# Turning a recurrence's outputs between the last gate tiles instead of behind them

## The chip, the cores and the metric

The kernel runs on one core of one Trainium2 chip. The metric is the device time of one execution in microseconds (us); a kernel's time is the median of its runs.

## The reference, cut to what matters

A first block mixes 512 tokens of width 1024 in four branches, gates and adds them, and is followed by two further layers. The change lies in branch A, a recurrence over four heads of 64 columns, and in what happens to its outputs:

```python
o = wkv7(rh, heads(decay), kh, vh, -kk, kk * ah)
o = layer_norm(o, lnx_w.reshape(H_A, HEAD_A), lnx_b.reshape(H_A, HEAD_A), LNX_EPS)
o = o + jnp.sum(rh * kh * r_k, axis=-1, keepdims=True) * vh
return (o.reshape(bsz, seq, D_MIX) * g) @ w_out, v_first
...
merged = (gates[:, :, 0] * y_a + gates[:, :, 1] * y_b + gates[:, :, 2] * y_c + gates[:, :, 3] * y_d)
x = x + gt1 * (merged @ w_o[l])
```

The norm is over the 64 columns of a head, for each token and head; its weight and bias are one number for each of the 256 columns.

## The kernel before

Activations lie with columns on the 128 partitions and 512 tokens in the free dimension. A matrix product is done in pieces: a piece is 1024 columns of weights for 128 partitions (512 KB), which makes one output tile of 128x512 from 8 blocks of 128 rows, or four output tiles from 2 blocks each (the branches' own output weights). Each block takes three products (high times high, high times low, low times high; L1602, in product_steps), so a piece is 24 products of 512 columns. Output tiles go round four PSUM banks, 0 to 3; a tile waits until its bank was read.

The weights come over GpSimd's queue in the order of the pieces, into four slots: load_high fetches a piece (L440), load_low negates it into the low half (L446) and adds it again by an accumulating transfer (L449). The first product of a piece frees the slot of the piece before it, and load_high of the third piece ahead waits for that; GpSimd works in order, so the low half of the piece after next is issued only behind it.

Ahead of the recurrence, blocks (L1916) does small products of 128 rows and 64 columns of weights, with outputs on the lower and the upper 64 partitions in turn. The recurrence goes over 16 chunks of 32 tokens (VectorE's loop L711, TensorE's with L1961 to L1982). Between its small products TensorE does gate tiles and branch tiles in steps (the generator named beside, L1937), and VectorE the gating of finished tiles in steps of its own (beside, L691, called by step_beside, L703). In VectorE's case 32 steps are to be done in 40 calls, so the last eight calls do nothing. ScalarE copies each chunk's outputs out of PSUM into the tile o (L1433), which has (head, token in the chunk) on the 128 partitions and (chunk, column) in the free dimension: 128x1024.

Behind the recurrence, TensorE does four gate tiles (project(4, "gate"), L1987), called gate tiles 1 to 4 here. Meanwhile VectorE norms o: mean, centred o, square, variance (L735 to L740), ScalarE's square root (L1468, in order behind the gate tiles left from the recurrence), reciprocal and scaling (L742, L743), then the norm's weight and bias, which lie repeated over 64 columns each in the tile vec (L746, L747). Then o is written twice, masked by the parity of the head (L750), and 32 TensorE products with 64 rows and 128 columns of weights, moved by 32 columns, turn it to columns on partitions (L1993; 64 instructions, since a product in plain float32 is two). VectorE adds the bonus, multiplies by g and splits into a high and a low half, for two tiles of 128x512 (L753, L754, L481, L482). This is the tail.

Then branch_out(3, 8) (L1998) makes the branch's eight output tiles from two pieces, here output pieces 1 and 2. VectorE gates each (L1112), adds it to the sum of the branches (L1121) and splits the sum in two (L481, L482), 4 instructions for each of 8 tiles. The first tile of the next projection (w_o, L1999) takes these halves as they come, and the other seven follow. SyncE fetches x again in four parts as the sum's tiles are done (L410).

Of the kernel before, what the change touches and what calls it, by code (L numbers as in the profile page):

```python
# [20 lines left out]
AX = mybir.AxisListType  # L21

P = 128
T = 512
# [3 lines left out]
H_A, HD = 4, 64  # L28
C = 32
NCK = T // C  # L30
# [57 lines left out]
def vec_columns():  # L88

    sizes = [("c", 8), ("ada_b", 48), ("g_mix", 8), ("mu", 7), ("w0", 2), ("a0", 2), ("kk", 2), ("ka", 2), ("rk", 2),  # L90
             ("sg_w", 2), ("sg_b", 2), ("conv_w", 6), ("s5_d", 2), ("a_re", 8), ("a_im", 8), ("log_dt", 8),
             ("g_ffn", 8), ("g_final1", 8), ("g_mix2", 16), ("g_mem2", 16), ("g_ffn2", 16), ("b_f", 1),
             ("cw2", 2 * 3 * 44), ("cb2", 2 * 44), ("g_final", 8), ("lnx_w", 64), ("lnx_b", 64)]
    at, cols = 0, {}
    for name, n in sizes:
        cols[name] = (at, n)
        at += n
    return cols, at


VEC, NVEC = vec_columns()


# [67 lines left out]
def build(nc, A, out):  # L171
# [15 lines left out]
    with ExitStack() as ctx:  # L187
# [5 lines left out]
        def S(name):  # L193
            if name not in sems:
                sems[name] = ctx.enter_context(nc.semaphore(name))
            return sems[name]
# [4 lines left out]
        x = sb("x", [P, KT, T])  # L201
        h_hi = sb("h_hi", [P, KT, T], F32R)
        h_lo = sb("h_lo", [P, KT, T], F32R)
        g_hi = sb("g_hi", [P, KT, T], F32R)
        g_lo = sb("g_lo", [P, KT, T], F32R)
        work = sb("work", [P, 6, T])
        vec = sb("vec", [P, NVEC])
        con = sb("con", [P, NCON])
        mod = sb("mod", [P, 48])
        small = sb("small", [P, 40, 8])  # L210
# [7 lines left out]
        ps = [banks8[:, i, :] for i in range(8)]  # L218
# [13 lines left out]
        def K(name):  # L232
            at, size = CON[name]
            return con[:, at:at + size]

        def place(sizes, at=0):

            parts = {}
            for name, shape in sizes:
# [7 lines left out]
                elif len(shape) == 4:  # L247
# [7 lines left out]
        rw_pad = place([("a", (2, NCK, 2, C)), ("b", (2, NCK, 2, C)), ("k", (2, NCK, 2, C)), ("r", (2, NCK, 2, C)),  # L255
                        ("g", (2, T)), ("bonus", (2, T))])
# [6 lines left out]
        rw_sol = place([("as", (C, C)), ("z", (C // 2, C)), ("o", (NCK, 64))],  # L263
                       at=max(rw_in["end"], rw_bd["end"]))
# [10 lines left out]
                     at=base_at + 7 * T)  # L275
# [9 lines left out]
                          at=sol_at))  # L285
# [181 lines left out]
        def _(dve):  # L467
            n = Counts()

            def do(ins, name="dve_step"):  # L470

                ins.then_inc(S(name), 1)
                dve.wait_ge(S(name), n.next(name))

            def need(name, by=1):

                dve.wait_ge(S(name), n.next(name, by))

            def both_parts(hi, lo, src, name):

                do(dve.tensor_copy(hi, src))  # L481
                do(dve.tensor_tensor(lo, src, hi.bitcast(F32), ALU.subtract), name)  # L482
# [112 lines left out]
            def vector_recurrence():  # L595

                v, bd, sol = rw_in, rw_bd, rw_sol
# [93 lines left out]
                def beside():  # L691

                    skip(8)
                    for f in range(4):
                        yield from gate_steps(4 + f)
                    for f in range(KT):
                        if f % 2 == 0:
                            skip(1)
                        yield from gate_steps(f, glu_tiles=True)

                steps, turn = beside(), [0]

                def step_beside():  # L703

# [24 lines left out]
                    pass  # L729
                need("rec_o")  # L730
                need("rec_o_copied", 2 * NCK)
                o, sq = sol["o"], bd["ab"]
                mean, var = small[:, 29:31, :].rearrange("p a b -> p (a b)"), small[:, 31:33, :].rearrange("p a b -> p (a b)")
                spread = lambda s: s.unsqueeze(2).broadcast_to((P, NCK, HD))
                do(dve.tensor_reduce(mean, o, AX.X, ALU.add))  # L735
                do(dve.tensor_scalar(mean, mean, 1.0 / HD, None, ALU.mult))
                do(dve.tensor_tensor(o, o, spread(mean), ALU.subtract))
                do(dve.tensor_tensor(sq, o, o, ALU.mult))
                do(dve.tensor_reduce(var, sq, AX.X, ALU.add))
                do(dve.tensor_scalar(var, var, 1.0 / HD, LNX_EPS, ALU.mult, ALU.add), "rw_var")  # L740
                need("rw_std")
                do(dve.reciprocal(var, var))  # L742
                do(dve.tensor_tensor(o, o, spread(var), ALU.mult))  # L743
                at_w, at_b = VEC["lnx_w"][0], VEC["lnx_b"][0]
                over = lambda at: vec[:, at:at + HD].unsqueeze(1).broadcast_to((P, NCK, HD))
                do(dve.tensor_tensor(o, o, over(at_w), ALU.mult))  # L746
                do(dve.tensor_tensor(o, o, over(at_b), ALU.add))  # L747
                opad = rw_pad["a"].rearrange("p a n h c -> p (a n h c)").rearrange("p (n h i) -> p n h i", n=NCK, h=2)
                for g in range(2):
                    do(dve.tensor_scalar(opad[:, :, g, :], o, K("hm")[:, g:g + 1], None, ALU.mult), "o_padded")  # L750
                for k in range(2):
                    need("rw_o")
                    do(dve.tensor_tensor(rw_pad["bonus"][:, k], rw_pad["bonus"][:, k], ps[4 + k][:], ALU.add))  # L753
                    do(dve.tensor_tensor(rw_pad["bonus"][:, k], rw_pad["bonus"][:, k], rw_pad["g"][:, k], ALU.mult))  # L754
                    both_parts(g_hi[:, 6 + k, :], g_lo[:, 6 + k, :], rw_pad["bonus"][:, k], "rw_out")
                skip(8)

            def vector_layer(layer):
# [257 lines left out]
            f = [blocks4(m["f"][:, part]) for part in range(2)]  # L1016
# [51 lines left out]
            while L < NQ:  # L1068
                over = lambda v: v.unsqueeze(2).broadcast_to((P, S5T, L))
# [505 lines left out]
        def _(pe):  # L1575
            n = Counts()
            piece, t = [0], [0]
# [71 lines left out]
            h = (of(h_hi), of(h_lo))  # L1649

            def project(tiles, owner, operand=h, width=T, blocks=8, ready=None):

                for i in range(tiles):
                    slot = open_piece()
                    product(slot, blocks, *operand, owner if isinstance(owner, str) else owner[i], width,
                            ready=ready if i == 0 else None)
# [157 lines left out]
            for k in range(2):  # L1814
                mm = pe.matmul(PA[:], K("ones"), m["z"][:, 2 + k, :], start=(k == 0), stop=(k == 1))
            mm.then_inc(S("sg_sums"), 1)
            project(1, "s5_u")
            for k in range(2):
                need("sg_square")
                mm = pe.matmul(PB[:], K("ones"), m["sq"][:, k, :], start=(k == 0), stop=(k == 1))  # L1820
            mm.then_inc(S("sg_sums"), 1)
            project(1, "dve_freed")
            for k in range(2):
                need("sg_normed")
                for b in range(QB):
                    mm = pe.transpose(ps[6 + k][:, P * b:P * b + P], m["z"][:, 2 + k, P * b:P * b + P], K("ident"))
# [16 lines left out]
            for s in range(S5T):  # L1843
                for part in range(2):
                    for g in range(2):
                        mm = pe.matmul(ps[4 + part][halves[g], NQ * s:NQ * s + NQ], m["e"][:, part, s, halves[g]], m["u_turned"][:, 2 * s + g, :],
                                       start=True, stop=True)
# [3 lines left out]
            for s in range(S5T):  # L1851
                for g in range(2):
                    pe.matmul(ps[6 + g][:, NQ * s:NQ * s + NQ], m["toep"][:, 2 * s + g].rearrange("p j c -> p (j c)"), m["u_turned"][:, 2 * s + g, :],
                              start=(s == 0), stop=False, skip_group_check=True)
            need("s5_states")
            for s in range(S5T):
                for part in range(2):
                    for g in range(2):
                        mm = pe.matmul(ps[6 + g][:, NQ * s + 1:NQ * s + NQ], m["g"][halves[g], part, s, :],
                                       m["w"][halves[g], part, NQ * s:NQ * s + NQ - 1], start=False,  # L1860
                                       stop=(part == 1 and s == S5T - 1), skip_group_check=True)
# [122 lines left out]
                next(steps, None)  # L1984
            for _ in steps:
                pass
            project(4, "gate")  # L1987
            pe.wait_ge(S("o_padded"), 2)
            opad = rw_pad["a"].rearrange("p a n h c -> p (a n h c)").rearrange("p (n x) -> p n x", n=NCK)
            for p in range(2):  # L1990
                rows = slice(64 * p, 64 * p + 64)
                for c in range(NCK):
                    mm = pe.matmul(ps[4 + p][:, C * c:C * c + C], opad[rows, c, :], K("sum32")[rows, :], start=True, stop=True)  # L1993
                mm.then_inc(S("rw_o"), 1)


            pe.wait_ge(S("rw_out"), 2)
            branch_out(3, 8)  # L1998
# [71 lines left out]
def columns(v):  # L2070

    return v.reshape(-1, P).T
# [34 lines left out]
def layout(i):  # L2107
# [21 lines left out]
    for layer, w in ((0, i["w_in_fox_2"][0]), (1, i["w_in_dil_2"][0])):  # L2129
# [14 lines left out]
        for n in FF2_GROUPS:  # L2144
# [11 lines left out]
           "b_f": np.concatenate([i["b_forget_2"][0], np.zeros(P - NH, np.float32)])[:, None],  # L2156
           "cw2": columns(i["conv_w_2"].reshape(-1)), "cb2": columns(i["conv_b_2"].reshape(-1)),
           "g_final": columns(i["norm_final_2"]),
           "lnx_w": np.repeat(f["rwkv_lnx_w"].reshape(H_A, HD), C, axis=0), "lnx_b": np.repeat(f["rwkv_lnx_b"].reshape(H_A, HD), C, axis=0)}
    b = np.stack([f["s5_b_re"], f["s5_b_im"]])  # L2160
    c = np.stack([f["s5_c_re"], f["s5_c_im"]])
    arrays = dict(
# [20 lines left out]
```

## Time and profile before

| | us |
|---|---|
| median of three runs | 2294.26 (2290.89 to 2295.56) |
| the profiled execution | 2292.73 |
| its span, first to last instruction | 2290.7 |
| TensorE busy | 2137.2, 93% of the span |
| VectorE busy | 1297.5, 57% |
| GpSimd busy | 843.6, 37% |
| ScalarE busy | 455.8, 20% |
| mean granted TensorE clock | 0.964 of full speed |

Rows give start and duration in us from the start of the span. A line L1602 is a line of the kernel, and stands for every call of a helper that it belongs to. The idle time in square brackets is that of the engine just before the instruction, with what ended it. TensorE (PE) overlaps its products, so the step from one start to the next tells its pace, not the duration; weight loads have rows of their own (PEld). Granted clock 1.00 is 2.4 GHz and 0.50 is 1.2 GHz.

### The profile page before, as it was taken

What the parts mean: (1) busy time and instruction counts of PE and PEld (TensorE: products, weight loads), DVE (VectorE), ACT (ScalarE), POOL (GpSimd) and SP (SyncE); (2) the same over time, 40 slices, a digit from 0 to 9 for tenths busy, and PEclk for the clock granted to TensorE, in tenths of its full rate; (3) what the DMA queues carried; (4) which work ended last, traced back from release to release, by engine and by line L of the source; (5) the groups of instructions that cost most, each with busy time, mean ns of one, the idle gap of its engine ahead of it and who ended that gap; (6) DMA issues with size and microseconds to landing.
All of it is one profiled execution on the core that took longest, in us unless ns stands there. A gap on an engine that the chain in (4) does not pass through costs nothing.

```text
span 2290.7 us, 27377 instructions
## 1 busy us (share of the span) xinstructions
PE 2137.2 (93%) x10790; PEld 1697.7 (74%) x10790; DVE 1297.5 (57%) x1824; ACT 455.8 (20%) x839; POOL 843.6 (37%) x1009
## 2 busy tenths in 40 slices
PE   6989799998799999989999999999989979999996
PEld 4768586676588888876767888888766658888885
DVE  7775655436763243684444754737746656727365
ACT  2112301220100000213332211102223432202011
POOL 1323233332244444442213444444432224444442
PEclk7999899998899999999999999999999989999998
DMA  8868577576799899975437889888964538888885
GB/s 289 231 134 173 114 142 148 120 175 167 237 233 195 191 198 190 194 170 127 102 74 171 188 192 195 189 197 170 201 134 100 103 81 187 189 196 192 194 186 126
DMA packets 121783, 389.40 MB, mean 170 GB/s; under 512 B 25220, under 2 KB 27396, under 8 KB 121272
## 3 DMA queue, kind: packets, MB, share of 16 engines
q0 software_dynamic: 96624, 346.27, 69.8%
q1 hardware_dynamic: 25032, 41.39, 5.4%
q8 instruction: 86, 1.41, 0.2%
q14 instruction: 41, 0.34, 0.1%
HBM read 383.73 MB, written 3.92 MB: 169 GB/s over the span
## 4 chain that ended last, share of the span: by engine, by line
PE 79%; DVE 12%; DMA 5%; issue 1%; ACT 1%; POOL 1%; SPq 0%; DVEq 0%; ACTq 0%
PE ps L1602 65%; DMA w_lo<-in_w 2%; PE ps L1730 2%; PE ps L1631 2%; PE ps L1759 2%; DMA arena<-in_ada 1%; PE ps L1745 1%; PE ps L1916 1%; DMA w_hi<-in_w 1%; DVE work L688 1%; DVE g_lo L482 1%; DVE arena L689 1%; DVE small L875 1%; DVE work L536 1%; DVE h_lo L532 0%
## 5 line engine op out<-in xcount | busy, mean ns | idle before, releaser
L1602 PE MATMUL ps<-h_hi,w_hi 128*128 128x512 f32 x1760 | 712.3, 405 | 28.7 <-DVE h_lo L532 13.3
L1602 PE MATMUL ps<-h_lo,w_hi 128*128 128x512 f32 x1760 | 691.0, 393 | 0.0
L1602 PE MATMUL ps<-h_hi,w_lo 128*128 128x512 f32 x1760 | 690.8, 392 | 0.0
L440 POOL DMA_DIRECT2D w_hi<-in_w x334 | 185.9, 557 | 1258.7 <-PE ps L1602 1190.4
L1602 PEld LDWEIGHTS ps<-h_hi,w_hi 128*128 128x128 f32 x1760 | 333.4, 189 | 127.5 <-issue 30.1
L1602 PEld LDWEIGHTS ps<-h_hi,w_lo 128*128 128x128 f32 x1760 | 333.3, 189 | 71.8
L1602 PEld LDWEIGHTS ps<-h_lo,w_hi 128*128 128x128 f32 x1760 | 334.0, 190 | 65.0 <-issue 2.2
L446 POOL TENSOR_SCALAR w_lo<-w_hi 128x1024 fp32r<-128x1024 f32 (+1 forms) x334 | 357.5, 1070 | 55.6 <-DMA w_hi<-in_w 50.2
L449 POOL DMA_DIRECT2D w_lo<-in_w x334 | 300.6, 900 | 105.7 <-POOL w_lo L446 105.7
L1602 PE MATMUL ps<-g_hi,w_hi 128*128 128x512 f32 (+1 forms) x792 | 310.9, 393 | 15.8 <-DVE g_lo L482 6.0
L1602 PE MATMUL ps<-g_lo,w_hi 128*128 128x512 f32 (+1 forms) x792 | 304.7, 385 | 0.0
L1602 PE MATMUL ps<-g_hi,w_lo 128*128 128x512 f32 (+1 forms) x792 | 304.5, 384 | 0.0
L1602 PEld LDWEIGHTS ps<-g_hi,w_hi 128*128 128x128 f32 x792 | 151.4, 191 | 51.2 <-DMA w_lo<-in_w 8.5
L1602 PEld LDWEIGHTS ps<-g_hi,w_lo 128*128 128x128 f32 x792 | 151.1, 191 | 29.5
L1602 PEld LDWEIGHTS ps<-g_lo,w_hi 128*128 128x128 f32 x792 | 151.4, 191 | 28.2 <-issue 0.5
L1560 ACT ACTIVATE arena<-arena,vec 128x512 f32<-128x512 f32 x88 | 71.8, 816 | 395.2 <-DVE arena L921 391.9
L935 DVE TENSOR_TENSOR x<-ps,x 128x512 f32<-128x512 f32 x48 | 33.2, 691 | 148.0 <-PE ps L1602 137.7
L921 DVE TENSOR_TENSOR arena<-ps,work 128x512 f32<-128x512 f32 x88 | 60.8, 691 | 94.8 <-PE ps L1602 93.4
L926 DVE SCALAR_TENSOR_TENSOR arena<-arena,vec 128x511 f32<-128x511 f32 x88 | 112.6, 1279 | 3.3 <-ACT arena L1560 0.3
L1190 DVE TENSOR_TENSOR arena<-arena 128x512 f32<-128x512 f32 x32 | 53.9, 1683 | 71.1 <-ACT arena L1481 71.1
L1198 DVE SCALAR_TENSOR_TENSOR x<-ps,mod,x 128x512 f32<-128x512 f32 x32 | 24.0, 750 | 102.2 <-PE ps L1602 102.1
L481 DVE CAST g_hi<-arena 128x512 fp32r<-128x512 f32 (+1 forms) x100 | 79.1, 791 | 3.4
(373 smaller groups left out, 2068.3 us busy)
## 6 DMA issues: line engine op xcount, KB each, us to landing
w_hi<-in_w POOLq DMA_DIRECT2D x318, 512.0 KB, 4.0
w_lo<-in_w POOLq DMA_DIRECT2D x318, 512.0 KB, 5.7
arena<-in_ada SPq DMA_DIRECT2D x40, 512.0 KB, 8.5
w_hi<-in_w POOLq DMA_DIRECT2D x16, 384.0 KB, 3.5
w_lo<-in_w POOLq DMA_DIRECT2D x16, 384.0 KB, 5.0
x<-in_ada SPq DMA_DIRECT2D x8, 512.0 KB, 7.2
x<-in_xT SPq DMA_DIRECT2D x1, 2048.0 KB, 9.9
x<-in_xT SPq DMA_DIRECT2D x4, 512.0 KB, 4.1
```

What stands on the lines that cost most here:

```text
L440: pool.dma_start(w_hi[:, q % SLOTS, 0:n], A["w"][q][:, 0:n]).then_inc(S(f"high_in{q % SLOTS}"), 16)
L446: pool.tensor_scalar(w_lo[:, q % SLOTS, 0:n], w_hi[:, q % SLOTS, 0:n].bitcast(F32), -1.0, 0.0, ALU.mult, ALU.add).then_inc(S("negated"), 1)
L449: pool.dma_start(w_lo[:, q % SLOTS, 0:n], A["w"][q][:, 0:n], accum_op=ALU.add).then_inc(S(f"low_in{q % SLOTS}"), 16)
L481: do(dve.tensor_copy(hi, src))
L921: do(dve.tensor_tensor(cv_m["z"][:, side, :], tile()[:], rstd, ALU.mult), "conv_scaled")
L926: do(dve.scalar_tensor_tensor(dst[:, 1:], z[:, :T - 1], w(1), dst[:, 1:], ALU.mult, ALU.add))
L1190: do(dve.tensor_tensor(s, r, r, ALU.mult), "relu_used")
L1560: do(act.activation(c[:, j % 2, :], cv_m["z"][:, side, :], ACT.Identity, scale=V("cw2", at), bias=V("cb2", 44 * layer + 22 * side + j0 + j ...
L1602: mm = pe.matmul(bank, w[:, slot, cols], a(k), start=(k == 0 and i == 0), stop=(k == blocks - 1 and i == 2))
L1631: mm = pe.matmul(banks[i], w[:, slots[i], cols], a(k), start=(k == 0 and j == 0), stop=(k == blocks - 1 and j == 2))
L1730: mm = pe.matmul(ps[2 + g][:, 0:width], at_m["q"][half(g), pair, P * qb:P * qb + P], keys, start=True, stop=not fox)
L1759: mm = pe.matmul(ps[6][64 * g:64 * g + 64, P * qb:P * qb + P], values, at_m["pt"][:, u % 2, g, P * b:P * b + P], start=(b == 0), stop=(b = ...
```

## The change

Three things are done. VectorE's steps beside the recurrence get four more: mean, centred o, square and sum of squares of chunks 0 to 7 (centred(0)); the same of chunks 8 to 15 follows the recurrence. The turning products move from behind gate tile 4 to behind gate tile 2, and take another form: o's 64 columns of one chunk, all 128 rows, are the weights, and the 64 columns of the identity that belong to one parity of heads are moved through; 32 products again, two for each chunk, with their outputs on the upper and the lower 64 partitions in turn. The masked copies of o (L750) fall away. The norm's weight and bias are one column each for the two tiles of the tail, where they ride on its instructions, and the tile vec is 124 columns narrower. The tail waits for all 32 products and then has, for each of two tiles, two instructions of 256 columns and one of 512 before the two of the split.

```diff
@@ vec_columns, L93
-             ("cw2", 2 * 3 * 44), ("cb2", 2 * 44), ("g_final", 8), ("lnx_w", 64), ("lnx_b", 64)]
+             ("cw2", 2 * 3 * 44), ("cb2", 2 * 44), ("g_final", 8), ("lnx_w", 2), ("lnx_b", 2)]
@@ vector_recurrence, L701
-                steps, turn = beside(), [0]
+                o, sq = sol["o"], bd["ab"]
...
+                def centred(first):
+                    at = slice(first, first + NCK // 2)
+                    dve.wait_ge(S("rec_o_copied"), 2 * (first + NCK // 2))
+                    do(dve.tensor_reduce(mean[:, at], o[:, at], AX.X, ALU.add))
+                    yield
+                    do(dve.tensor_scalar(mean[:, at], mean[:, at], 1.0 / HD, None, ALU.mult))
+                    do(dve.tensor_tensor(o[:, at], o[:, at], mean[:, at].unsqueeze(2).broadcast_to((P, NCK // 2, HD)), ALU.subtract))
+                    yield
+                    do(dve.tensor_tensor(sq[:, at], o[:, at], o[:, at], ALU.mult))
+                    yield
+                    do(dve.tensor_reduce(var[:, at], sq[:, at], AX.X, ALU.add))
+                    yield
+                def all_beside():
+                    yield from beside()
+                    yield from centred(0)
+                steps, turn = all_beside(), [0]
@@ vector_recurrence, L732 to L755
-                do(dve.tensor_reduce(mean, o, AX.X, ALU.add))
-                do(dve.tensor_scalar(mean, mean, 1.0 / HD, None, ALU.mult))
-                do(dve.tensor_tensor(o, o, spread(mean), ALU.subtract))
-                do(dve.tensor_tensor(sq, o, o, ALU.mult))
-                do(dve.tensor_reduce(var, sq, AX.X, ALU.add))
+                for _ in centred(NCK // 2):
+                    pass
                 do(dve.tensor_scalar(var, var, 1.0 / HD, LNX_EPS, ALU.mult, ALU.add), "rw_var")
                 need("rw_std")
                 do(dve.reciprocal(var, var))
-                do(dve.tensor_tensor(o, o, spread(var), ALU.mult))
...
-                do(dve.tensor_tensor(o, o, over(at_w), ALU.mult))
-                do(dve.tensor_tensor(o, o, over(at_b), ALU.add))
-                opad = rw_pad["a"].rearrange("p a n h c -> p (a n h c)").rearrange("p (n h i) -> p n h i", n=NCK, h=2)
-                for g in range(2):
-                    do(dve.tensor_scalar(opad[:, :, g, :], o, K("hm")[:, g:g + 1], None, ALU.mult), "o_padded")
+                do(dve.tensor_tensor(o, o, var.unsqueeze(2).broadcast_to((P, NCK, HD)), ALU.mult), "o_normed")
+                need("rw_o", 2)
                 for k in range(2):
-                    need("rw_o")
-                    do(dve.tensor_tensor(rw_pad["bonus"][:, k], rw_pad["bonus"][:, k], ps[4 + k][:], ALU.add))
-                    do(dve.tensor_tensor(rw_pad["bonus"][:, k], rw_pad["bonus"][:, k], rw_pad["g"][:, k], ALU.mult))
-                    both_parts(g_hi[:, 6 + k, :], g_lo[:, 6 + k, :], rw_pad["bonus"][:, k], "rw_out")
+                    bonus = rw_pad["bonus"][:, k]
+                    for q in range(2):
+                        part = slice(T // 2 * q, T // 2 * q + T // 2)
+                        do(dve.scalar_tensor_tensor(bonus[:, part], ps[4 + q][:, T // 2 * k:T // 2 * k + T // 2], V("lnx_w", k), bonus[:, part],
+                                                    ALU.mult, ALU.add))
+                    do(dve.scalar_tensor_tensor(bonus, bonus, V("lnx_b", k), rw_pad["g"][:, k], ALU.add, ALU.mult))
+                    both_parts(g_hi[:, 6 + k, :], g_lo[:, 6 + k, :], bonus, "rw_out")
@@ TensorE's program, L1987 to L1997
-            project(4, "gate")
-            pe.wait_ge(S("o_padded"), 2)
-            opad = rw_pad["a"].rearrange("p a n h c -> p (a n h c)").rearrange("p (n x) -> p n x", n=NCK)
-            for p in range(2):
-                rows = slice(64 * p, 64 * p + 64)
-                for c in range(NCK):
-                    mm = pe.matmul(ps[4 + p][:, C * c:C * c + C], opad[rows, c, :], K("sum32")[rows, :], start=True, stop=True)
+            project(2, "gate")
+            pe.wait_ge(S("o_normed"), 1)
+            for q in range(2):
+                for c in range(NCK // 2):
+                    for g in range(2):
+                        columns_of = K("ident").rearrange("r (p h t) -> r p h t", p=2, h=2)[:, :, g, :]
+                        place_of = ps[4 + q][64 * g:64 * g + 64, :].rearrange("i (p n t) -> i p n t", p=2, t=C)[:, :, c, :]
+                        mm = pe.matmul(place_of, rw_sol["o"][:, NCK // 2 * q + c, :], columns_of, start=True, stop=True)
                 mm.then_inc(S("rw_o"), 1)
-
+            project(2, "gate")
```

## Rows read from the trace of the kernel before

**Rows 1.** The page: the chain that ended last, its shares of the span by engine.

```profile
PE 79%; DVE 12%; DMA 5%; issue 1%; ACT 1%; POOL 1%; SPq 0%; DVEq 0%; ACTq 0%
```

**Rows 2.** The chain of waits, 470 to 560 us: start us, us, what.

```profile
492.91 9.32 DMA w_lo<-in_w
...
502.27 16.66 PE ps L1602 x72
518.93 7.91 PE ps L1993 x64
...
556.17 4.21 PE ps L1602 x9
```

**Rows 3.** TensorE's timeline, 492 to 543 us: start us, us, engine, line, operation, [idle before, releaser].

```profile
507.66 0.39 PE L1602 MATMUL ps<-h_hi,w_lo 128*128 128x512 f32 x1
...
518.54 0.39 PE L1602 MATMUL ps<-h_hi,w_lo 128*128 128x512 f32 x1
...
529.58 0.80 PE L1602 MATMUL ps<-g_hi,w_hi 128*128 128x512 f32 x1 [2.76 <-DVE g_lo L482]
...
534.80 0.40 PE L1602 MATMUL ps<-g_hi,w_hi 128*128 128x512 f32 x1
```

**Rows 4.** Stretches: length, busy PE, PEld, DVE, ACT, POOL, granted clock, DMA share, GB/s.

```profile
304.00:306.00 2.00, 2.00 (x25) 1.67 (x20) 1.48 (x3) 0.00 (x0) 0.57 (x2) 1.00 0.81 213
...
524.00:525.00 1.00, 1.00 (x9) 1.00 (x8) 0.93 (x3) 0.00 (x0) 0.00 (x0) 0.74 0.00 0
```

**Rows 5.** TensorE's timeline at two groups of small products, 276 to 282 and 301 to 330 us.

```profile
277.13 3.68 PE L1916 MATMUL ps<-arena 128*64 128x64 f32 x64 [16.62 <-DVE arena L652]
...
302.40 2.09 PE L1916 MATMUL ps<-arena 128*64 128x64 f32 x64
304.42 0.50 PE L1602 MATMUL ps<-h_hi,w_hi 128*128 128x512 f32 x1
```

**Rows 6.** Line L1982 in the recurrence: duration ns min/median/max, first and last start, forms.

```profile
L1982 PEld LDWEIGHTS ps<-work,arena x52: 132/134/136, 406.2 to 487.7; 128*64 128x64 f32 x52
L1982 PE MATMUL ps<-work,arena x52: 222/246/270, 406.2 to 487.8; 128*64 128x64 f32 x52
```

**Rows 7.** VectorE's timeline, 486 to 560 us.

```profile
497.37 0.25 DVE L742 RECIPROCAL small<-small 128x16 f32<-128x16 f32 x1 [2.53 <-ACT small L1468]
497.65 1.23 DVE L743 TENSOR_TENSOR arena<-arena,small 128x1024 f32<-128x1024 f32 x1
...
526.92 0.69 DVE L753 TENSOR_TENSOR arena<-arena,ps 128x512 f32<-128x512 f32 x1 [1.60 <-PE ps L1993]
...
528.37 0.43 DVE L481 CAST g_hi<-arena 128x512 fp32r<-128x512 f32 x1
...
532.60 0.69 DVE L1112 TENSOR_TENSOR work<-ps,arena 128x512 f32<-128x512 f32 x1 [3.08 <-PE ps L1602]
...
546.37 1.83 DVE L482 TENSOR_TENSOR h_lo<-x,h_hi 128x512 fp32r<-128x512 f32 x1
...
555.42 0.69 DVE L482 TENSOR_TENSOR h_lo<-x,h_hi 128x512 fp32r<-128x512 f32 x1
559.97 0.75 DVE L1173 SCALAR_TENSOR_TENSOR x<-ps,mod,x 128x512 f32<-128x512 f32 x1 [3.86 <-DMA x<-in_xT]
```

**Rows 8.** GpSimd's timeline, 486 to 560 us.

```profile
510.52 0.89 POOL L449 DMA_DIRECT2D w_lo<-in_w  x1 [0.30 <-POOL w_lo L446]
...
530.68 0.55 POOL L440 DMA_DIRECT2D w_hi<-in_w  x1 [13.83 <-PE ps L1602]
...
546.59 1.06 POOL L446 TENSOR_SCALAR w_lo<-w_hi 128x1024 fp32r<-128x1024 f32 x1
```

**Rows 9.** VectorE's timeline in the recurrence's last steps.

```profile
478.54 0.22 DVE L719 COPY work<-ps 64x64 f32<-64x64 f32 x1 [1.63 <-PE ps L1969]
```

**Rows 10.** The page: DMA issues, KB each, median us from issue to landing.

```profile
w_lo<-in_w POOLq DMA_DIRECT2D x318, 512.0 KB, 5.7
...
vec<-in_vec SPq DMA_DIRECT2D x1, 335.0 KB, 2.9
```

More of the change, by code:

```diff
@@ L699, in beside @@
                         yield from gate_steps(f, glu_tiles=True)
-                steps, turn = beside(), [0]
+                o, sq = sol["o"], bd["ab"]
+                mean, var = small[:, 29:31, :].rearrange("p a b -> p (a b)"), small[:, 31:33, :].rearrange("p a b -> p (a b)")
+                def centred(first):
[14 more added lines that the diff above has]
+                steps, turn = all_beside(), [0]
                 def step_beside():
@@ L731, in vector_recurrence @@
                 need("rec_o_copied", 2 * NCK)
-                o, sq = sol["o"], bd["ab"]
-                mean, var = small[:, 29:31, :].rearrange("p a b -> p (a b)"), small[:, 31:33, :].rearrange("p a b -> p (a b)")
-                spread = lambda s: s.unsqueeze(2).broadcast_to((P, NCK, HD))
-                do(dve.tensor_reduce(mean, o, AX.X, ALU.add))
-                do(dve.tensor_scalar(mean, mean, 1.0 / HD, None, ALU.mult))
-                do(dve.tensor_tensor(o, o, spread(mean), ALU.subtract))
-                do(dve.tensor_tensor(sq, o, o, ALU.mult))
-                do(dve.tensor_reduce(var, sq, AX.X, ALU.add))
+                for _ in centred(NCK // 2):
+                    pass
                 do(dve.tensor_scalar(var, var, 1.0 / HD, LNX_EPS, ALU.mult, ALU.add), "rw_var")
@@ L742, in vector_recurrence @@
                 do(dve.reciprocal(var, var))
-                do(dve.tensor_tensor(o, o, spread(var), ALU.mult))
-                at_w, at_b = VEC["lnx_w"][0], VEC["lnx_b"][0]
-                over = lambda at: vec[:, at:at + HD].unsqueeze(1).broadcast_to((P, NCK, HD))
-                do(dve.tensor_tensor(o, o, over(at_w), ALU.mult))
-                do(dve.tensor_tensor(o, o, over(at_b), ALU.add))
-                opad = rw_pad["a"].rearrange("p a n h c -> p (a n h c)").rearrange("p (n h i) -> p n h i", n=NCK, h=2)
-                for g in range(2):
-                    do(dve.tensor_scalar(opad[:, :, g, :], o, K("hm")[:, g:g + 1], None, ALU.mult), "o_padded")
-                for k in range(2):
-                    need("rw_o")
-                    do(dve.tensor_tensor(rw_pad["bonus"][:, k], rw_pad["bonus"][:, k], ps[4 + k][:], ALU.add))
-                    do(dve.tensor_tensor(rw_pad["bonus"][:, k], rw_pad["bonus"][:, k], rw_pad["g"][:, k], ALU.mult))
-                    both_parts(g_hi[:, 6 + k, :], g_lo[:, 6 + k, :], rw_pad["bonus"][:, k], "rw_out")
+                do(dve.tensor_tensor(o, o, var.unsqueeze(2).broadcast_to((P, NCK, HD)), ALU.mult), "o_normed")
+                need("rw_o", 2)
+                for k in range(2):
+                    bonus = rw_pad["bonus"][:, k]
[5 more added lines that the diff above has]
+                    both_parts(g_hi[:, 6 + k, :], g_lo[:, 6 + k, :], bonus, "rw_out")
                 skip(8)
@@ L2158, in layout @@
            "g_final": columns(i["norm_final_2"]),
-           "lnx_w": np.repeat(f["rwkv_lnx_w"].reshape(H_A, HD), C, axis=0), "lnx_b": np.repeat(f["rwkv_lnx_b"].reshape(H_A, HD), C, axis=0)}
+           "lnx_w": columns(f["rwkv_lnx_w"].reshape(-1)), "lnx_b": columns(f["rwkv_lnx_b"].reshape(-1))}
     b = np.stack([f["s5_b_re"], f["s5_b_im"]])
```

## The prediction

> **What bounds the kernel now.** I read the chain of waits first. TensorE holds 79% of it and VectorE 12% [rows 1], so a change counts where TensorE stands still, runs slowly, or hands the chain to VectorE. All three happen behind the recurrence [rows 2]. A late weight transfer, 9.32 us long, holds gate tile 2 until 502.27. The gate tiles follow at 10.88/48 = 0.227 us a product, from the last product of tile 2 at 507.66 to the last of tile 4 at 518.54 [rows 3]. Then the 64 turning instructions take 7.91 us, to 526.84 [rows 2], 0.124 us each; TensorE stands 2.76 us for the tail on VectorE, and output piece 1 starts at 529.58 [rows 3]. The clock has been lost meanwhile: its mean is 0.74 in the sixth microsecond of the turning products [rows 4], and output piece 1's first product takes 0.80 us where the thirteenth, at 534.80, takes 0.40 [rows 3]. The twelve before that took 5.22 us instead of 12 x 0.227 = 2.72. VectorE gates the first output tile at 532.60 and from there holds the chain itself: its last instruction of the stretch ends at 555.42 + 0.69 = 556.11 [rows 7], and TensorE goes on at 556.17 [rows 2]. So the figure to follow is the 532.60. What comes after it hangs on events, not on a fixed time.
>
> **The turning products, moved and made anew.** Their new form has 128 rows, 64 columns of weights and 64 moved columns, with outputs on the two halves of the partitions in turn. The trace has just this shape at L1916: 64 instructions at 302.40, the next gate tile's product at 304.42, so 2.02 us [rows 5], with the clock at 1.00 behind them [rows 4]. New are a moving operand and an output in two runs of 32 columns; no row shows what that costs. Above, 7.91 us, today's form, bounds it; below, the 2.02 themselves, since split runs can hardly beat whole ones of the same shape and count. I take 2.02, the nearest row.
>
> The Trainium skill speaks against so low a price: "TensorE: Matmul & The Clock Gate", Back-to-back issue gap, gives a product of up to 64 columns about 62 ns where instructions are decoded in microcode. That would make 64 x 62 ns = 4.0 us, and the sum 2 us worse. L1916's 2.02/64 = 32 ns says that this does not bind here [rows 5].
>
> So the products start behind gate tile 2, at 507.66 + 0.39 = 508.05, and end at 510.07. They wait for the normed o, ready at 497.65 + 1.23 = 498.88 [rows 7], 9.2 us early. Gate tiles 3 and 4 then take 10.88 us and a first step about 0.1 longer: output piece 1 can start at 521.05, 8.5 us sooner. Of this 5.9 are the cheaper products and 2.7 the tail's wait, less that step.
>
> **The tail under gate tiles 3 and 4.** It begins at about 510.2 and has, for each of two tiles, two instructions of 256 columns, one of 512, a cast of 0.43 and a subtraction of 0.69 [rows 7]. The one with 512 is 0.75, by the same operation on PSUM at 559.97. Those of 256 lie between nothing and 0.75; I take 0.48. With gaps a tile is 3.0 us and the tail 6.0, done at 516.2, under cover until 521.05. GpSimd's negation can stretch a VectorE instruction from 0.69 to 1.83, as at 546.37 beside the one at 546.59 [rows 7, 8]; two such make 518.5, still covered. Without the cover the tail would cost its 6 us.
>
> **The clock.** With gate tiles right ahead, output piece 1 runs at full clock. VectorE got its first tile 3.02 us behind the piece's start; six products at 0.227, the last 0.39 long, and 0.1 for the signal make 1.6. VectorE starts at 522.7: 9.9 us sooner.
>
> **VectorE's stretch.** It took 23.5 us and still has its 32 instructions. Two of them were stretched by 1.14; a third negation came at 530.68 + 0.55 = 531.2 [rows 8], just before it. Now it comes at about 522.3 (1.1 + 0.55 behind output piece 1's start, less 0.4 for that product at full clock) and falls on the stretch's first two instructions. Nothing to +1.14; I take +0.6.
>
> For that third one the Trainium skill has a rule in "SBUF — State Buffer", Who interferes with whom: a VectorE instruction with at most one input in SBUF, outside the two-port modes, doesn't contend with GpSimd. The first, L1112, reads PSUM and SBUF and would go free, and the sum would be 0.6 better if the negation ended with it; no row settles the second.
>
> **The norm's halves.** Four new steps in VectorE's program fall into calls that did nothing. Each is half of an instruction of about 1.2 us, and VectorE stands 1.63 us at such a place [rows 9]. Should one be stretched, what queues behind it is a copy that TensorE reads only after six more products, 1.4 us. Cost nothing; bound from above 1 us. The gain is nothing too: the reciprocal waits for ScalarE's root [rows 7], which is in order behind a gate tile, and the normed o has 9.2 us to spare. L746, L747 and L750 fall away under the same cover.
>
> **Weights.** Output piece 1's low half is issued about 2.6 us behind the start of gate tile 3 (510.52 against 507.89) [rows 8] and lands in 5.7 [rows 10]: 8.3 us, where the new order leaves 11.0. With the 9.32 of rows 2 it would be 1 us late. The wait before gate tile 2 stays; shorter VectorE work beside GpSimd's negation might cut its 1.8 us, and a busier one lengthen it; I take nothing. The vec transfer is 124 of 670 columns shorter. Of its 2.9 us [rows 10] that is at most 0.5; I take 0.2, since other loads share the queue.
>
> **Sum.** -9.9 + 0.6 - 0.2 = -9.5 us, made against the profiled execution of 2292.73: 2283.2. The median of the runs is 1.5 above it, so 2284.8 on that base; I forecast 2284, between the two.
>
> **Rivals.**
> *The clock falls under the small products.* The same 64 instructions took 3.68 us at 277.13, where TensorE came from 16.62 us of idling [rows 5]. Then +1.7 here, and +2.5 for the first twelve products behind. For it: the turning products lost the clock in their sixth microsecond [rows 4]. Against: these last 2, and L1916 kept it. 2288.2.
> *Products as dear as today*, because of the split runs: 7.91 us, the clock lost as now. Output piece 1 at 508.05 + 7.91 + 11.0 + 2.5 = 529.5, as before; only the first tile's clock is won, 1.4, and 0.2 at the start, less 0.6: -1.0, so 2292.5.
> *Slower: the products don't overlap at all.* A weight load of this shape lasts 0.134 and a product 0.246 [rows 6]; one after the other 64 take 24.3 us, and the end comes 22.3 later than forecast: 2306. The change loses from about 11.5 us (2.0 + 9.5), 0.18 us an instruction. For it: the same weights go to both halves in a row, which no row here shows. Against: L1916 alternates halves too, at 0.032.
> *The gain is partly given back in weights.* GpSimd idled 13.83 us before 530.68 [rows 8], waiting for TensorE; that rest shrinks, and three pieces could each be 1 us late. Against: the slack of 2.7 above. 2287.
> *A fixed price for each small instruction*, of the 57 ns that they had in 277.13's group (3.68/64), the clock kept behind them: +1.7, 2285.7. Against: the group at 302.40. This case stands for the rule of "TensorE: Matmul & The Clock Gate" in the Trainium skill, above.
>
> **How the numbers follow.** Forecast 0.70; clock 0.08; dear products 0.07; no overlap 0.04; weights 0.07; the fixed price 0.04. A measurement of this kernel tells a change of 0.2%, 4.6 us, from none: faster is below 2289.7. The forecast and the cases up to 2288.2 hold 0.89, of which 0.04 lies too near the bound: faster 0.85, same 0.11 with the dear products, slower 0.04. Range: below, a cheaper start (0.3), no third stretch (0.6), up to 1.8 from the wait before gate tile 2, and the spread of the runs: 2280. Above, up to the clock rival: 2289.
>
> **What would show it.** The turning products in some 2 us right behind gate tile 2 at clock 1.00, no wait of output piece 1 for g_lo, its first product at 0.39 to 0.5 us, the tail over some 5 us earlier, and VectorE's stretch beginning about 9.9 us sooner. Wrong would be: turning products above 4 us, a clock of 0.5 in gate tile 3, a wait for w_lo before output piece 1 or 2, longer recurrence steps, or the 9 us missing again further on.

## The result, and the profile after

| | before | after |
|---|---|---|
| median, us | 2294.40 (2290.89 to 2295.56, 4 runs) | 2277.22 (2275.16 to 2282.63, 4 runs) |
| ratio, 95% interval | | 0.9928 [0.9911, 0.9946] |
| profiled execution, its span | 2292.73, 2290.7 | 2276.95, 2275.1 |

The changed kernel is faster by 17.2 us, where 10 were forecast; 2277.22 lies below the range of 2280 to 2289. A second series of six runs gave a smaller gain, 14.6 us: 2280.84 against 2295.39, ratio 0.9936 [0.9917, 0.9954]. Among the runs of all experiments one, of the kernel with a wide vec, was in a slower state (3067.55 us) and is left out of its median.

The chain of waits of the changed kernel, start and duration in us, answers to [rows 2]:

```profile
491.15 8.23 DMA w_lo<-in_w
...
499.43 5.74 PE ps L1615 x24
505.16 2.02 PE ps L2007 x64
507.18 20.64 PE ps L1615 x90
527.82 0.70 DVE work L1125
...
542.16 14.19 PE ps L1615 x52
```

The turning products (now L2007) lie between the gate tiles and take 2.02 us. The 90 products behind them, gate tiles 3 and 4 and output pieces 1 and 2, follow without the wait for VectorE that stood at 526.84 to 529.58 before. VectorE takes the chain at 527.82, and TensorE goes on at 542.16, where it went on at 556.17 before. The wait for the low weight half, which lasted 1.78 us before, is 0.15 here; gate tile 2's first products, before and after:

```profile
502.27 0.50 PE L1602 MATMUL ps<-h_hi,w_hi 128*128 128x512 f32 x1 [1.78 <-DMA w_lo<-in_w]
```

```profile
499.43 0.50 PE L1615 MATMUL ps<-h_hi,w_hi 128*128 128x512 f32 x1 [0.15 <-DMA w_lo<-in_w]
```

TensorE's timeline at the turning products and at the start of output piece 1, and the stretches around them (granted clock behind the sixth time) answer to [rows 3, 4]:

```profile
505.09 2.08 PE L2007 MATMUL ps<-con,arena 128*64 128x64 f32 x64
507.11 0.50 PE L1615 MATMUL ps<-h_hi,w_hi 128*128 128x512 f32 x1
...
518.12 0.39 PE L1615 MATMUL ps<-g_hi,w_hi 128*128 128x512 f32 x1
```

```profile
505.00:507.00 2.00, 2.00 (x65) 1.91 (x64) 0.00 (x0) 0.60 (x1) 0.00 (x0) 1.00 0.95 147
507.00:509.00 2.00, 2.00 (x15) 1.63 (x11) 1.63 (x3) 0.00 (x0) 1.07 (x2) 1.00 0.69 133
518.00:520.00 2.00, 2.00 (x11) 1.65 (x10) 0.26 (x1) 1.60 (x2) 1.17 (x2) 1.00 0.96 184
```

Clock 1.00 throughout, and output piece 1 starts with a product of 0.39 us and no wait. VectorE's timeline answers to [rows 7], GpSimd's negations to [rows 8]:

```profile
496.43 1.23 DVE L759 TENSOR_TENSOR arena<-arena,small 128x1024 f32<-128x1024 f32 x1
507.30 1.00 DVE L765 SCALAR_TENSOR_TENSOR arena<-ps,vec,arena 128x256 f32<-128x256 f32 x2 [9.64 <-PE ps L2007]
508.33 1.76 DVE L767 SCALAR_TENSOR_TENSOR arena<-arena,vec 128x512 f32<-128x512 f32 x1
...
513.75 1.81 DVE L482 TENSOR_TENSOR g_lo<-arena,g_hi 128x512 fp32r<-128x512 f32 x1
519.74 0.69 DVE L1125 TENSOR_TENSOR work<-ps,arena 128x512 f32<-128x512 f32 x1 [4.18 <-PE ps L1615]
...
525.02 0.69 DVE L1125 TENSOR_TENSOR work<-ps,arena 128x512 f32<-128x512 f32 x1
...
532.37 1.83 DVE L482 TENSOR_TENSOR h_lo<-x,h_hi 128x512 fp32r<-128x512 f32 x1
...
541.42 0.69 DVE L482 TENSOR_TENSOR h_lo<-x,h_hi 128x512 fp32r<-128x512 f32 x1
545.99 0.75 DVE L1186 SCALAR_TENSOR_TENSOR x<-ps,mod,x 128x512 f32<-128x512 f32 x1 [3.88 <-DMA x<-in_xT]
```

```profile
519.38 1.07 POOL L446 TENSOR_SCALAR w_lo<-w_hi 128x1024 fp32r<-128x1024 f32 x1
...
524.83 1.07 POOL L446 TENSOR_SCALAR w_lo<-w_hi 128x1024 fp32r<-128x1024 f32 x1
...
532.58 1.07 POOL L446 TENSOR_SCALAR w_lo<-w_hi 128x1024 fp32r<-128x1024 f32 x1
```

The normed o is ready at 496.43 + 1.23 = 497.66, the turning products start at 505.09. The tail runs from 507.30 to 513.75 + 1.81 = 515.56, 8.3 us with two stretched instructions, and still ends 2.6 us ahead of output piece 1 at 518.12. The first gating comes at 519.74, 1.62 us behind the piece's start (3.02 before). From there to the end of the last low half it is 22.37 us (23.51 before): one instruction stretched to over 1.8 us, at 532.37, instead of two. The one of before that [rows 7] doesn't show, with its negation:

```profile
538.60 1.85 DVE L1121 TENSOR_TENSOR x<-x,work 128x512 f32<-128x512 f32 x1
```

```profile
538.84 1.07 POOL L446 TENSOR_SCALAR w_lo<-w_hi 128x1024 fp32r<-128x1024 f32 x1
```

### The profile page after: what moved, and what is told of

Same layout as the page of the kernel before. It is cut to its first block, busy times and chain, and to the rows that moved or that the text cites. A ratio compares the mean times of both kernels' runs of the same rounds, so it can differ in the third digit from the quotient of the medians.

```text
span 2275.1 us, 27381 instructions
## 1 busy us (share of the span) xinstructions
PE 2129.2 (94%) x10790; PEld 1689.9 (74%) x10790; DVE 1297.9 (57%) x1827; ACT 456.1 (20%) x839; POOL 846.9 (37%) x1009
## 3 DMA queue, kind: packets, MB, share of 16 engines
q8 instruction: 86, 1.41, 0.3%
## 4 chain that ended last, share of the span: by engine, by line
PE 79%; DVE 13%; DMA 4%; issue 1%; ACT 1%; POOL 0%; SPq 0%; DVEq 0%; ACTq 0%
PE ps L1615 66%; DMA w_lo<-in_w 2%; PE ps L1743 2%; PE ps L1644 2%; PE ps L1772 2%; PE ps L1758 1%; DMA w_hi<-in_w 1%; DVE work L688 1%; PE ps L1929 1%; DVE arena L689 1%; DMA arena<-in_ada 1%; DVE g_lo L482 1%; DVE small L888 1%; DVE work L536 1%; DVE h_lo L532 0%
```

## The experiments

To keep the place apart from everything else, each profile is read in a local stretch: from the end of the recurrence's last instruction on VectorE to the first update of x. Before it was 559.97 - 488.05 = 71.92 us, after 545.99 - 486.85 = 59.14. The recurrence's last instructions, before and after:

```profile
487.45 0.60 DVE L725 SCALAR_TENSOR_TENSOR work<-ps,small,work 128x64 f32<-128x64 f32 x2 [1.91 <-PE ps L1976]
```

```profile
486.25 0.60 DVE L747 SCALAR_TENSOR_TENSOR work<-ps,small,work 128x64 f32<-128x64 f32 x2 [1.91 <-PE ps L1989]
```

The ratios are to the kernel before as it was timed beside each kernel, at 2295.39 or 2295.49 us; the first row's median is that of the first series.

| kernel | local stretch, us | recurrence ends at | median, ratio |
|---|---|---|---|
| before, first profile | 71.92 | 488.05 | 2294.40 |
| before, second and third | 71.65, 71.88 | 487.03, 484.50 | |
| halves alone, two profiles | 70.32, 71.78 | 490.72, 493.71 | 2294.15, 0.9995 [0.9983, 1.0007] |
| old form in the new place | 68.82 | 490.17 | 2291.90, 0.9982 [0.9967, 0.9997] |
| new form in the old place | 67.23 | 485.70 | 2287.50, 0.9966 [0.9951, 0.9980] |
| after, two profiles | 59.14, 58.70 | 486.85, 487.73 | 2280.84, 0.9936 [0.9917, 0.9954] |
| after with a wide vec, two profiles | 58.72, 58.69 | 484.68, 492.33 | 2281.08, 0.9927 [0.9906, 0.9949] |
| after with the whole norm | 59.12 | 487.29 | |
| after, products twice | 61.32 | 485.22 | |
| after, high halves by ScalarE | 57.43 | 487.57 | 2278.96, 0.9923 [0.9905, 0.9941] |

**The changed kernel again**, no edit.

> The changed kernel again, as the base of the others. Theory A: some 10 us of the gain are made between gate tile 2 and the first gating on VectorE, as predicted (turning products 2.0 us instead of 7.9, tail covered, clock kept), 1 to 3 us come from the weight wait before gate tile 2 and from one stretched VectorE instruction fewer, and the 1 us ahead of the place and the 1.5 us far behind it are scatter between executions. Then this run shows the turning products again in 2.0 us and the first gating 12 to 13 us ahead of the kernel before, and a total gain of 13 to 17 us. Rival L: the shorter vec tile, which shifts every tile behind it in memory, makes the rest of the kernel faster as well; then the 2.5 us outside the place come back in this run.

Turning products in 2.02 us again, first gating at 520.20, local stretch 58.70. The total gain was 14.6 us, inside theory A's 13 to 17. The recurrence ended 0.3 us earlier than before, and the part behind the local stretch took 2281.6 - 546.43 = 1735.2 us against 1730.7: nothing gained outside the place in this execution.

**A vec as wide as before.**

```diff
-  ("lnx_w", 2), ("lnx_b", 2)]
+  ("lnx_w", 2), ("lnx_b", 2), ("pad", 124)]
```

> The changed kernel with 124 unused columns behind the last ones of vec, so that the transfer and the places of all later tiles are those of before. Theory A: the same as the changed kernel within 1 us. Rival L: 2 to 3 us slower than the changed kernel, spread over the whole span.

2281.08, 0.2 us from the changed kernel in the same series: no effect of the narrower tile can be seen. That speaks against rival L, but the two ratios' intervals reach some 4 us to each side, so they don't exclude its 2 to 3 us.

**The new form in the old place.**

```diff
-            project(2, "gate")
+            project(4, "gate")
             pe.wait_ge(S("o_normed"), 1)
...
-            project(2, "gate")
```

> The new form of the turning products, but behind gate tile 4 as before. Theory A: the products still take 2.0 us, but the tail is open: it waits for all products and needs some 6.5 us, TensorE stands that long, loses the clock and does output piece 1's first products at half of it (+1.4 until the first gating). 7 to 9 us slower than the changed kernel, so 6 to 9 faster than before. Rival F (the form alone makes the gain, the cover is worth little): within 3 us of the changed kernel.

The local stretch is 67.23, 8.1 to 8.5 longer than after (6.7 in the total). Its chain of waits:

```profile
514.65 2.04 PE ps L2007 x64
...
516.78 0.49 DVE arena L765
...
522.08 0.70 DVE g_lo L482
...
522.83 11.92 PE ps L1615 x42
```

The products take 2.04 us, then the open tail runs from 516.78 to 522.78: 6.0 us without a stretched instruction, as the prediction's sum had it. TensorE's wait for it is 6.16 us, longer than the 2.76 of [rows 3], since the new tail cannot start with the first half. Rival F falls: in the local stretch the form alone (with all of the change but the place) is worth some 4 us of 12.6. In the medians it is more, 7.9 of 14.6 us (2295.39 - 2287.50); the local figure is from one profile, and what makes the difference is open.

**The old form in the new place.**

```diff
-            project(4, "gate")
+            project(2, "gate")
             pe.wait_ge(S("o_padded"), 2)
...
+            project(2, "gate")
             pe.wait_ge(S("rw_out"), 2)
```

> The kernel before with its turning products, its masked copies and its tail as they were, but between gate tiles 2 and 3. Theory A: the products take 7 to 8 us, the clock falls behind their fifth microsecond and gate tile 3 begins at half of it (+2.5), while the tail is covered: 7 to 9 us slower than the changed kernel. Rival P (the place alone makes the gain): within 3 us of the changed kernel, with products of about 2 to 4 us.

The chain of waits, and the stretches around the turning products (columns as above):

```profile
490.12 18.21 PE ps L1602 x78
508.34 10.06 PE ps L1993 x64
518.40 22.21 PE ps L1602 x90
```

```profile
508.00:510.00 2.00, 2.00 (x18) 1.74 (x16) 0.00 (x0) 0.60 (x1) 0.00 (x0) 1.00 0.93 174
510.00:512.00 2.00, 2.00 (x22) 2.00 (x22) 0.00 (x0) 0.00 (x0) 0.00 (x0) 0.88 0.98 195
512.00:514.00 2.00, 2.00 (x14) 2.00 (x13) 1.45 (x3) 0.00 (x0) 0.00 (x0) 0.50 0.04 8
...
521.00:523.00 2.00, 2.00 (x9) 1.60 (x8) 1.04 (x2) 0.00 (x0) 0.96 (x2) 0.81 0.72 238
```

Here the old products take 10.06 us, more than theory A's 7 to 8, and the clock is gone sooner than in the first profile: it averages 0.88 over 510 to 512, is 0.50 from 512 on, and comes back only in gate tile 3. So the kernel is 10 us slower than the changed one in the local stretch and 11 in the total, more than theory A's 7 to 9. The tail is covered, but the lost clock gives part of that back; 2.7 us are left. Rival P falls. In the local stretch form and place gain 4.3 and 2.7 us apart, and 12.6 together: the form leaves TensorE a longer wait for the tail, which only the place covers, and the place pays for a lost clock, which only the form keeps. The medians give 7.9 and 3.5 apart and 14.6 together, the same way but by 3 us only, which their intervals do not tell from nothing.

**The kernel before, profiled again**, no edit.

> The kernel before, profiled once more, to learn which parts of its time between the recurrence's end and the first update of x come back. Theory A (the wait for the low half of gate tile 2's weights, 1.8 us in the first profile, is scatter): the wait is away or of another size, and the stretch from the recurrence's end to the first update of x is 70.1 us instead of 71.9. Rival W (the wait belongs to the order of before): it is there again with 1.5 us or more. Turning products 7.9 us and output piece 1's first products at half clock by both.

No wait for weights, yet the same local stretch of 71.65. Its chain and its clock say why:

```profile
487.88 28.11 PE ps L1602 x123
515.99 9.43 PE ps L1993 x64
...
528.17 12.35 PE ps L1602 x42
```

```profile
519.00:523.00 4.00, 4.00 (x29) 4.00 (x28) 2.50 (x4) 0.00 (x0) 0.00 (x0) 0.61 0.02 5
523.00:525.00 2.00, 2.00 (x11) 2.00 (x11) 0.00 (x0) 0.00 (x0) 0.00 (x0) 0.50 0.00 0
```

The turning products take 9.43 us instead of the 7.91 of [rows 2], because the clock falls earlier in them: 0.61 over 519 to 523, which are their fourth to seventh microseconds. So theory A was right about the wait, but its 70.1 us and the 7.9 us of the products did not come back. The first profile showed the products cheap and the weights late; the two nearly cancelled in its local stretch.

**The whole norm behind the recurrence.**

```diff
                     yield from beside()
-                    yield from centred(0)
...
-                for _ in centred(NCK // 2):
-                    pass
+                do(dve.tensor_reduce(mean, o, AX.X, ALU.add))
+                do(dve.tensor_scalar(mean, mean, 1.0 / HD, None, ALU.mult))
+                do(dve.tensor_tensor(o, o, spread(mean), ALU.subtract))
+                do(dve.tensor_tensor(sq, o, o, ALU.mult))
+                do(dve.tensor_reduce(var, sq, AX.X, ALU.add))
```

> The changed kernel without the halves: mean, centred o, square and variance of all 16 chunks behind the recurrence, as before. Theory A: nothing changes; the normed o is ready some 7 us or more before the turning products start, and the stretch from the recurrence's end to the first update of x stays at 58.7 to 59.2 us, with at most a scattered weight wait. Rival H (the shorter VectorE work beside GpSimd's negation is what removed the weight wait): the wait of 1.5 to 2 us before gate tile 2 is back.

59.12, as after, and no wait for weights. VectorE's timeline:

```profile
496.61 0.25 DVE L761 RECIPROCAL small<-small 128x16 f32<-128x16 f32 x1 [2.52 <-ACT small L1484]
496.89 1.23 DVE L762 TENSOR_TENSOR arena<-arena,small 128x1024 f32<-128x1024 f32 x1
507.61 1.00 DVE L768 SCALAR_TENSOR_TENSOR arena<-ps,vec,arena 128x256 f32<-128x256 f32 x2 [9.49 <-PE ps L2010]
```

The normed o is ready at 496.89 + 1.23 = 498.12, 10.8 us behind the recurrence's end, just as in the changed kernel with its halves: ScalarE's root, for which the reciprocal waits, sets it in both (496.15 there, behind 4.10 us of waiting). The turning products start 7.3 us later. Rival H falls.

**The halves alone**, in the kernel before, run twice.

```diff
+                def all_beside():
+                    yield from beside()
+                    yield from centred(0)
...
-                do(dve.tensor_reduce(mean, o, AX.X, ALU.add))
...
+                for _ in centred(NCK // 2):
+                    pass
```

> The kernel before with the halves alone: the norm of chunks 0 to 7 in the recurrence's last steps, everything else as it was. Theory A: no gain; the recurrence's steps keep 6.78 us each, and the stretch from its end to the first update of x is that of before, 70 to 72 us. Rival H: the weight wait is gone for that reason, 1.8 us less.

> The kernel before with the halves alone, timed. Theory A (the norm has time to spare): the same as before within 2 us. Rival H (the halves carry part of the gain): 2 to 4 us faster than before.

Local stretches 70.32 and 71.78, and 2294.15 against 2295.49, ratio 0.9995: no gain. The first of the two profiles alone would have suited rival H, with 0.18 us of weight wait and a local stretch 1.6 us below 71.92; but the kernel before has profiles without the wait too, and the turning products, 8.02 us in the first, took 10.44 in the second.

**The turning products twice**, writing the same again.

```diff
-            for q in range(2):
+            for q in (0, 1, 0, 1):
...
-                mm.then_inc(S("rw_o"), 1)
+            mm.then_inc(S("rw_o"), 2)
```

> The changed kernel with its turning products done twice, the second time writing the same. Theory A: they lie on TensorE's path at 2.0 us, so the first gating comes 2.0 us later, with the clock at 1.00 through gate tile 3. Rival C (more small products lose the clock): 4 us of them at the end and output or gate tiles at half clock, 4 us or more later. Rival N (they lie beside a wait): no later.

The chain of waits, and the stretches beside the products:

```profile
503.86 3.88 PE ps L2007 x128
507.74 20.64 PE ps L1615 x90
```

```profile
505.00:507.00 2.00, 2.00 (x76) 2.00 (x74) 0.00 (x0) 0.00 (x0) 0.00 (x0) 1.00 0.77 152
507.00:509.00 2.00, 2.00 (x32) 1.71 (x29) 1.07 (x3) 0.00 (x0) 0.53 (x1) 1.00 0.15 31
```

3.88 us for 128 instructions, clock 1.00 in the gate tile behind. The local stretch is 2.2 to 2.6 us longer, 0.5 of it a weight wait. So the products do lie on the path at 2 us, and even 4 us of them kept the clock in this one profile: rivals C and N fall.

**High halves of the sum by ScalarE**, a version that might beat both.

```diff
-                both_parts(h_hi[:, f, :], h_lo[:, f, :], merged[:, f, :], "merged")
+                do(dve.tensor_tensor(merged[:, f, :], merged[:, f, :], product, ALU.add), "summed")
+                if f:
+                    merged_low(f - 1)
...
+            for f in range(KT):
+                need("summed")
+                do(act.activation(h_hi[:, f, :], merged[:, f, :], ACT.Copy), "sum_high")
```

> The changed kernel, with the high half of the branches' sum (eight casts of 128x512 to h_hi) made by ScalarE instead of VectorE, and VectorE's subtraction for a tile put behind the next tile's sum. Theory A (VectorE's stretch from the first gating to the last low half sets the end, 32 instructions in 22.4 us with one stretched): 8 x 0.47 us less on VectorE, some 0.8 us more at the end for ScalarE's last copy, so the stretch takes about 19.4 us and the first update of x comes 3 us sooner after the recurrence's end, at some 55.8 instead of 58.9 us. Rival D (transfers of the next stage set the time behind it): the same 3 us there, but the total moves by less than 1 us. Rival S (ScalarE or the hand-over is slower than the cast): the stretch is as long as before or longer.

VectorE's and ScalarE's timelines:

```profile
521.74 0.69 DVE L1186 TENSOR_TENSOR work<-ps,arena 128x512 f32<-128x512 f32 x1 [4.18 <-PE ps L1627]
...
526.81 1.62 DVE L1181 TENSOR_TENSOR h_lo<-x,h_hi 128x512 fp32r<-128x512 f32 x1
...
538.79 1.48 DVE L1181 TENSOR_TENSOR h_lo<-x,h_hi 128x512 fp32r<-128x512 f32 x2
545.00 0.75 DVE L1195 SCALAR_TENSOR_TENSOR x<-ps,mod,x 128x512 f32<-128x512 f32 x1 [4.73 <-DMA x<-in_xT]
```

```profile
523.25 0.63 ACT L1498 ACTIVATE h_hi<-x 128x512 fp32r<-128x512 f32 x1 [2.27 <-DVE x L1188]
```

The stretch from the first gating to the last low half fell to 540.27 - 521.74 = 18.5 us from 22.4, although two instructions were stretched. The last part of x then took 4.7 us to come instead of 3.9. The local stretch is 57.43, of which 1.41 was a weight wait before gate tile 2: some 2.9 us less than after without that wait, and 1.4 with it. In the total, 2278.96 cannot be told from the changed kernel's 2277.22 and 2280.84, so rival D is neither shown nor excluded.

**Scatter ahead of the place.**

> The kernel before, profiled a third time. In the first two and in its variant with the halves alone the recurrence ended at 487.0 to 490.7 us, in the six kernels with the new turning products at 484.7 to 487.7. Theory A (scatter of weight transfers ahead of the place, which the change doesn't touch): this run ends its recurrence somewhere from 484 to 491. Rival L (something of the change makes the part ahead 2 to 3 us faster): 487.5 or later. From there to the first update of x 70 to 72 us.

> The changed kernel with vec as wide as before, profiled a second time; up to the recurrence's last three chunks it is the kernel before, in every transfer and place. Theory A: the recurrence ends anywhere from 484 to 491 us, and from there to the first update of x it takes 58.7 to 59.2 us. Rival L: it ends at 487.5 or later.

The kernel before ended its recurrence at 484.50, where rival L needs 487.5 or later. The changed one with a wide vec ended it at 492.33, later than theory A's 491 and by itself in line with rival L, but in its first profile it had ended at 484.68. So the scatter of one program is larger than the shift that rival L asks for. Over all 14 profiles the six with the narrow vec end at 485.2 to 487.7, 486.7 on average, and the eight with the wide one at 484.5 to 493.7, 488.9 on average: a shift of 2 us is neither shown nor excluded. Local stretches 71.88 and 58.69.

## Why the prediction was right or wrong

**Right:** the mechanism and its order. The products took 2.02 us, the row of L1916, and split runs cost nothing; the doubled products show that this is a price on the path. The rule of the Trainium skill that would have made it 4.0 us ("TensorE: Matmul & The Clock Gate", Back-to-back issue gap) doesn't bind here, at 32 ns an instruction. The tail went under gate tiles 3 and 4; two stretched instructions made it 8.3 us, and the bound of 518.5 for its end had allowed for just two. A 256-column instruction cost 0.49, taken as 0.48. The clock stayed at 1.00, and the first gating came 1.62 us behind output piece 1's start, taken as 1.6. The halves were worth nothing that the runs show. The start term of 0.2 for vec is too small to be found in any total: its transfer took 2.7 us in the profile after, 2.9 before [rows 10].

**Wrong: the size.** The local stretch lost 12.6 us (71.5 on average over the five profiles of before and of the halves alone, 58.9 over the five of after, with the wide vec and with the whole norm), not the 9.3 of the sum without its start term. The second series' 2280.84 lies just inside the range, but its gain of 14.6 us is too large for the sum as well. Three terms failed.

*"Nothing to +1.14; I take +0.6" for VectorE's stretch.* It became shorter: 22.36 or 22.37 us in all five profiles of after, against 22.6 to 23.6 in the five of before, 23.3 on average. I had seen only that a third negation now fell into the stretch. In the changed kernel two of the three fall on the gating instruction (519.38 on 519.74, 524.83 on 525.02), and both of these took 0.69. The gating reads PSUM and one tile in SBUF; the Trainium skill's rule in "SBUF — State Buffer", Who interferes with whom, which would let it go free, agrees. One negation of three hit a subtraction, 1.83. So the term was -0.9 on average in place of +0.6, off by 1.5 us. It goes with the place: the old form in the new place had 22.36 as well, the new form in the old place 23.18. Where output piece 1 starts at full clock the first negation begins some 0.36 us ahead of the first gating; in the first profile of before it began 1.35 ahead (531.25 on 532.60), and the next one fell on L1121.

*"The wait before gate tile 2 stays", taken as nothing.* It was 1.78 us in the execution I read, and over 1 us in only 2 of 14 profiles; both orders have executions without it. I took a thing of one execution for one of the kernel, and with "nothing" I set no gain for its going, though the range held one of up to 1.8. On average it was 0.4 us in the five profiles of before (1.78 and 0.18 in two of them) and 0.03 in those of after.

*"5.9 are the cheaper products."* The old ones took 7.9 us in that execution, and 8.0 to 10.4 in five other profiles of them, depending on when the clock fell. 7.91 was the lowest of six. Over the five profiles of the local stretch they average 9.1, so the saving was 7.1, 1.2 more. With the stretch's 1.5 and the weight wait's 0.4 that makes 3.1 of the 3.3 us from 9.3 to 12.6; the last 0.2 is not assigned.

**What stays open.** The total moved by 17.2 and 14.6 us in two series, 2 to 4.6 more than the local stretch. Outside it the time scatters: the recurrence ended between 484.5 and 493.7 us, even in one program 7.7 us apart (484.68 and 492.33), and from the first update of x to the end it took 1730.7 to 1734.8 us before and 1729.1 to 1735.2 after. Single runs of the changed kernel went from 2274.26 to 2283.85. A shift of 2 us, of the narrow vec or of anything else, can hide in that, and no run here shows a cause for one. What sets the moment at which the clock falls in the old products is open too. The range was too narrow for that as well: it gave the spread of the runs too little room beside the 1.8 us for the weight wait.

**The rivals.** No run showed a lost clock under the new products, products without overlap, or gain given back in weights: output pieces 1 and 2 waited for none in any profile of the changed kernel.

## What to carry to other kernels

Before a stall or a slow group is put into a sum, profile the same kernel twice: a wait for a transfer, and the point where the clock falls, can belong to one execution. Two edits that each win little can win much together when one opens what the other covers (4.3 and 2.7 us apart, 12.6 together in the local stretch here). The form of small products can matter more than their number: 0.032 us an instruction in the new form against 0.124 to 0.16 in the old, which ran in part at half clock. The forms differ in the rows and columns of weights, in the columns moved and in whether the outputs alternate between halves of the partitions; which of these counts was not tested. The cheap form was seen with full-width products right ahead; behind 16.62 us of idling the same shape took 3.68 us for 64 [rows 5].

## What was not expected of the hardware

The old turning products, 64 rows with 128 columns of weights each, lost the clock 2.8 to 5.6 us after their start in all six profiles of them, although TensorE never stood still; in the trace of before their starts lie 0.112 us apart while the clock is 1.00 and 0.213 at 0.50. 3.88 us of the new ones, right behind gate tiles in the same way, kept it at 1.00; that is shorter than the time that some of the old ones had, so how long the new form would keep it is not shown. And a VectorE instruction that reads PSUM passed GpSimd's negation unstretched twice in one stretch, while the subtraction of two tiles in SBUF beside it went from 0.69 to 1.83 us.
